# A 31-tap causal convolution with 16 taps on TensorE over stacked, shifted copies

## The chip, the cores and the metric

The kernel runs on one core of one Trainium2 chip. The metric is the device time in microseconds (us) of one execution. A core has TensorE (PE; its weight loads are shown apart as PEld), VectorE (DVE), ScalarE (ACT), GpSimd (POOL) and SyncE (SP). SP and ACT issue DMAs here. Engines wait for each other through semaphores only: `wait_ge(s, n)` holds an engine until semaphore `s` has reached `n`; a landed DMA adds 16, a finished instruction adds 1.

## The reference

Two decoder layers over 256 tokens of 1024 channels, all in float32. Layer 0 mixes tokens with a convolution module, layer 1 with sparse attention; each is followed by a mixture of 32 experts (two per token) and a gated embedding. The part that the change touches is the convolution module:

```python
def conv_module(xn, w_pw1, b_pw1, w_dw, b_dw, ln_g, ln_b, w_pw2, b_pw2):
    u = xn @ w_pw1 + b_pw1                     # 1024 -> 2048
    a, g = jnp.split(u, 2, axis=-1)
    u = a * jax.nn.sigmoid(g)                  # gated product
    u = lax.conv_general_dilated(              # 31 taps, each channel by itself
        u, w_dw[:, None, :].astype(u.dtype), window_strides=(1,),
        padding=[(CONV_WIDTH - 1, 0)], dimension_numbers=("NWC", "WIO", "NWC"),
        feature_group_count=u.shape[-1]) + b_dw
    u = jax.nn.silu(layer_norm(u, ln_g, ln_b))
    return u @ w_pw2 + b_pw2
```

## The kernel before

**Stages.** Norm of the input, conv module, mixture 0 with 32 experts of 6.3 MB each, embedding, attention, mixture 1, embedding. SP issues nearly all loads, in one order written out by hand; where a load goes over a buffer still in use, SP waits for its last reader. Each expert is three loads of 2 MB (gate, up, down) into one of two ring halves; inside the loop the gate and up loads wait for the gate and up products (`gu_mm`) of the expert before in that half, the down load for its down product (`y_mm`).

**Conv module.** Channels lie on partitions, in eight blocks of 128; tokens lie along the free axis. For each block c:
- PE computes pw1, 16 matmuls of 128x128 by 128x256 (L498). A float32 matmul shows as two records in the trace. After it, PE does the taps of block c-1 (`taps`, L477), and from block 3 on the channel sum of block c-3 (L483).
- ACT takes the sigmoid of the gate half (L1086) and builds six diagonal matrices, the identity times a tap weight (L1092).
- DVE forms the gated product into `cv0` (`glu`, L1324), a buffer with 30 columns of zeros in front, so that tap w of a block is a shifted view `cv0[:, c, w:w+256]`.
- The 31 taps are split. DVE does 20, each a multiply-add over a view, in two alternating accumulators (L1339, L1341, L1343). GpSimd does 5 (L990, L993, L994). PE does 6 (`PE_TAPS`), as matmuls with the diagonal matrices. DVE then adds the parts (L1353 to L1355).
- DVE's order is: taps of c, gated product of c+1, the adds of c (after PE's and GpSimd's parts), taps of c+1.

After block 7 PE puts the bias of pw2 into PSUM (L508, issued behind the last taps), finishes the channel sums and, with squares from ACT, the sums of squares (L513). DVE takes the mean at L1358. Then come square root, silu and pw2 (L522), 32 matmuls of 512 columns, and the router of mixture 0.

**The first loads.** SP: x; the vectors (biases, gains, the tap table `wdw_rows`, `bpw2`), which PE waits for before its first transposes (L461); pw1 in four parts (8 MB); pw2 (4 MB, L356); expert 0 (6 MB); after block 3 of pw1 two ple weights, after block 7 one attention weight and the gate weights of expert 1; after the last taps the embeddings; after pw2's products the up and down weights of expert 1. ACT first issues 14 small loads (router weights and biases, positions; L1066), then does its half of the norm (token tile 1; L1045, L1047, L1052).

## Time and profile before

| | us |
|---|---|
| median of 3 runs | 1414.63 (1410.31 to 1415.55) |
| the profiled execution | 1413.13 |
| its span | 1411.4 |
| PE busy | 1081.1 |
| DVE busy | 332.7 |
| ACT busy | 257.3 |
| POOL busy | 478.3 |

Mean DMA rate over the span: 318 GB/s, 447 MB read. The span is the time from the first to the last instruction of the profiled execution. In the rows below a timeline row gives start, duration, engine, line, operation, tiles and shapes and, in brackets, how long the engine stood idle before it and what ended that. "x32" means 32 instructions run together; their duration is that of the whole run. L numbers are lines of the kernel before.

### The profile page before, as it was taken

Reading aid. Unit: us, or ns where it says so; the run is one execution under the profiler, and the core shown is the slowest. Engines: PE = TensorE matmul, PEld = TensorE weight load, DVE = VectorE, ACT = ScalarE, POOL = GpSimd, SP = SyncE. Lnnn points to the kernel's source line nnn. Section 1 sums busy time; section 2 is a strip of 40 time slices with the busy share of each in tenths; the row PEclk is TensorE's granted clock in tenths of the full one; section 3 lists DMA queues with packets and bytes.
Section 4 is the critical chain, followed back from the end, with each engine's and each line's share of the span. In section 5 each row is a group of like instructions: output and inputs, shape, how many; then the busy total and the mean of one; then the engine's idle time right before and its main releaser. Section 6 shows DMA issues by size and latency. Waiting matters only on the chain.

```text
span 1411.4 us, 27617 instructions
## 1 busy us (share of the span) xinstructions
PE 1081.1 (77%) x10280; PEld 617.1 (44%) x10281; DVE 332.7 (24%) x917; ACT 257.3 (18%) x608; POOL 478.3 (34%) x793
## 2 busy tenths in 40 slices
PE   5985977776767777677999799877767677676768
PEld 4863454433433433343454554544334343333433
DVE  3997230000000000001407691300000000000011
ACT  2211131111111111111202481311111111111111
POOL 3663035334343343432000040363343333452520
PEclk9996989888888988888999899998988888888979
DMA  8922049999999999998303801799999999998940
GB/s 250 403 91 111 26 193 408 428 430 427 429 430 428 428 430 428 429 430 316 125 2 118 358 1 44 319 415 428 428 430 429 427 430 429 427 429 335 430 172 30
DMA packets 62731, 448.75 MB, mean 318 GB/s; under 512 B 10826, under 2 KB 21698, under 8 KB 38114
## 3 DMA queue, kind: packets, MB, share of 16 engines
q1 hardware_dynamic: 58114, 447.91, 76.5%
q10 hardware_dynamic: 4576, 0.30, 0.3%
q8 instruction: 26, 0.43, 0.1%
q14 instruction: 15, 0.12, 0.0%
HBM read 447.14 MB, written 1.05 MB: 318 GB/s over the span
## 4 chain that ended last, share of the span: by engine, by line
DMA 44%; PE 36%; DVE 6%; issue 3%; ACT 1%; SPq 1%; POOL 0%; DVEq 0%
DMA ring<-in_moe_w_up 42%; PE PS L547 14%; PE PS L437 9%; PE PS L522 2%; DMA ring<-in_moe_w_down 2%; PE PS L562 2%; PE PS L534 1%; PE PS L752 1%; PE PS L725 1%; PE PS L569 1%; SPq L310 1%; DVE ppw L1654 1%; PE PS L425 1%; PE PS L586 1%; DVE ppw L1679 1%
## 5 line engine op out<-in xcount | busy, mean ns | idle before, releaser
L547 PE MATMUL PS<-ring,arena 128*32 128x256 f32 x4128 | 347.4, 500 | 203.9 <-DMA ring<-in_moe_w_up 183.0
L547 PEld LDWEIGHTS PS<-ring,arena 128*32 128x32 f32 x4128 | 164.0, 138 | 376.4 <-issue 225.4
L1389 DVE TENSOR_TENSOR arena<-PS,arena 64x256 f32<-64x256 f32 x65 | 27.8, 428 | 634.7 <-ACT arena L1147 629.0
L562 PE MATMUL PS<-ring,arena 128*32 128x256 f32 x2080 | 125.7, 381 | 30.8 <-DVE arena L1392 30.8
L964 POOL TENSOR_SCALAR arena<-arena 128x32 f32<-128x32 f32 x64 | 18.8, 294 | 334.3 <-PE PS L534 330.8
L1147 ACT ACTIVATE arena<-PS 64x256 f32<-64x256 f32 x64 | 24.2, 378 | 546.6 <-PE PS L547 546.6
L923 POOL TENSOR_SCALAR arena<-arena 128x512 f32<-128x512 f32 x67 | 105.9, 1580 | 23.5 <-POOL arena L970 12.9
L562 PEld LDWEIGHTS PS<-ring,arena 128*32 128x32 f32 x2080 | 73.0, 109 | 61.2 <-issue 37.4
L917 POOL TENSOR_SCALAR arena<-arena 128x32 f32<-128x32 f32 x260 | 88.6, 364 | 13.1 <-POOL arena L964 12.9
L925 POOL TENSOR_TENSOR arena<-arena 128x512 f32<-128x512 f32 x67 | 85.3, 1273 | 5.6
L534 PE MATMUL PS<-hn,arena 128*32 128x256 f32 x1072 | 76.8, 399 | 8.4 <-DMA ring<-in_moe_w_down 7.8
L569 PE MATMUL PS<-arena 32*128 32x256 f32 x1040 | 74.5, 397 | 6.6 <-ACT arena L1145 0.6
L437 PE MATMUL PS<-wb,xnT 128*128 128x512 f32 x160 | 74.1, 621 | 0.0
L1384 DVE TENSOR_TENSOR arena<-PS,g 128x256 f32<-128x256 f32 x67 | 28.5, 425 | 177.9 <-PE PS L540 177.9
L912 POOL TENSOR_TENSOR rstd<-rstd,nhalf 128x1 f32<-128x1 f32 x12 | 8.2, 696 | 163.1 <-DVE rstd L1289 163.1
L970 POOL TENSOR_SCALAR arena<-arena 128x1 f32<-128x1 f32 x64 | 14.6, 228 | 138.3 <-PE PS L569 138.3
L569 PEld LDWEIGHTS PS<-arena 32*128 32x128 f32 x1040 | 50.3, 183 | 17.4 <-issue 17.4
L1151 ACT COPY arena<-PS 128x256 f32<-128x256 f32 x64 | 23.9, 374 | 162.9 <-PE PS L562 162.9
L534 PEld LDWEIGHTS PS<-hn,arena 128*32 128x32 f32 x1072 | 36.3, 110 | 35.2 <-issue 9.2
L927 POOL TENSOR_TENSOR arena<-arena 128x256 f32<-128x256 f32 x67 | 49.0, 731 | 5.2
L1147 ACT ACT_TABLE_LOAD x32 | 41.1, 1283 | 45.7 <-issue 45.7
L437 PEld LDWEIGHTS PS<-wb,xnT 128*128 128x128 f32 x160 | 31.6, 200 | 39.2 <-issue 39.2
(303 smaller groups left out, 1275.4 us busy)
## 6 DMA issues: line engine op xcount, KB each, us to landing
ring<-in_moe_w_up SPq DMA_DIRECT2D x64, 2048.0 KB, 23.1
ring<-in_moe_w_down SPq DMA_DIRECT2D x64, 2048.0 KB, 24.8
ring<-in_moe_w_gate SPq DMA_DIRECT2D x63, 2048.0 KB, 18.7
wb<-in_ple_w_gate SPq DMA_DIRECT2D x4, 2048.0 KB, 20.4
ring<-in_conv_w_pw SPq DMA_DIRECT2D x3, 2048.0 KB, 19.4
ring<-in_nsa_w_in SPq DMA_DIRECT2D x3, 2048.0 KB, 20.5
wb<-in_nsa_w_in SPq DMA_DIRECT2D x2, 2048.0 KB, 9.0
wb<-in_nsa_cmp_w SPq DMA_DIRECT2D x2, 2048.0 KB, 8.3
```

What stands on the lines that cost most here:

```text
L437: i = pe.matmul(PS[:, bank, :], lhs[:, k, t * P:(t + 1) * P], w[:, k, :], start=start and k == 0, stop=(k == KD - 1))
L522: i = pe.matmul(PS[:, 2 * n + t, :], cT[:, k, t * P:(t + 1) * P], dense(PW2[n])[:, k, :], start=False, stop=(k == KD - 1))
L534: i = pe.matmul(PS[32 * j:32 * j + 32, BGX, 0:Q4].rearrange("q (p c) -> q p c", c=2), lhs[:, t, :], rows[:, j], start=(t == 0), stop=(t == ...
L547: i = pe.matmul(PS[32 * j:32 * j + 32, BGU, 0:256].rearrange("q (p c) -> q p c", c=2), xT[:, k, :], w[:, k, :].rearrange("q (p h c) -> q h ...
L562: i = pe.matmul(PS[32 * j:32 * j + 32, BY, 0:Q4], hT[:, c, 32 * f:32 * f + 32], w_dn(s)[:, f, c, Q4 * j:Q4 * (j + 1)], start=(q == 0), sto ...
L569: i = pe.matmul(PS[:, ACC + j, 256 * t:256 * (t + 1)], w[32 * j:32 * j + 32, t * P:(t + 1) * P], ysb[32 * j:32 * j + 32, :], start=False, ...
L917: i = g.tensor_scalar(eq4[:, t, k, :], c32, S4[:, t, k:k + 1], None, ALU.is_equal)
L923: g.tensor_scalar(eqr, srow, cc, None, ALU.is_equal).then_inc(count, 1)
L925: g.tensor_tensor(eqr, eqr, wrow, ALU.mult).then_inc(count, 1)
L927: g.tensor_tensor(to, eqr[:, 0, :], eqr[:, 1, :], ALU.add).then_inc(ok, 1)
L1147: nc.scalar.activation(gs[64:128, :], PS[0:64, BGU, 0:256], ACT.Silu).then_inc(sil_ok, 1)
L1384: return v.tensor_tensor(dst.rearrange("p (j c) s -> p j c s", c=2), PS[:, BGX, Q4:Q4 + 256].rearrange("p (c j s) -> p j c s", c=2, j=4), ...
```

## The change

- `PE_TAPS` goes from 6 to 16, in stacks of 4 (`STACK`). GpSimd does no taps any more, and DVE does 15.
- For the taps on PE the gated product of a block is written by ACT to a DRAM tensor (`xdram`), ACT waits for that, and reads it back four times, each shifted by one token, so that 32 channels x 4 shifts fill the 128 partitions (`xst`, for four groups q of 32 channels). A matmul then has a 128x32 stationary matrix holding 4 taps of 32 channels, and writes 32 partitions; 4 groups x 4 runs make 16 matmuls for 16 taps of all 128 channels.
- The stationary matrices come from one GpSimd product per block (`stk` times `wst`), in place of ACT's six operations. Their tap weights are brought into stacked order once, through a second DRAM tensor (`wdram`).
- DVE adds two parts in place of three: first its two accumulators, then PSUM.
- In front, SP loads x, the vectors without `bpw2`, and pw1. pw2 goes out in four 1 MB pieces, each after the copies of one of the blocks 0 to 3 have landed; `bpw2` behind them. Expert 0 goes out after the copies of blocks 6 and 7 have landed, then the embeddings, the gate weights of expert 1, the two ple weights and the attention weight.
- ACT's small loads are issued behind the copies of blocks 2 to 5.
- PE waits for pw2 and `bpw2` before the bias matmuls, and for the embeddings with one semaphore.

```diff
-PE_TAPS, POOL_TAPS = 6, 5
+PE_TAPS, STACK = 16, 4
+RUNS = PE_TAPS // STACK
+DVE_TAPS = TAPS - PE_TAPS
+XW = T + STACK * (RUNS - 1)
...
+        xdram = nc.dram_tensor("glu_rows", (KD, P, T + STACK * RUNS - 1), F32, kind="Internal").ap()
+        wdram = nc.dram_tensor("tap_rows", (P, STACK * 8 * RUNS), F32, kind="Internal").ap()
...
             sp.dma_start(wdw_rows, conv_w_dw[0]).then_inc(vec_in, 16)
-            sp.dma_start(bpw2, conv_b_pw2).then_inc(vec_in, 16)
...
-            for n in range(2):
-                sp.dma_start(dense(PW2[n]), cols(conv_w_pw2[0], n)).then_inc(w2_in[n], 16)
+            for c in range(4):
+                sp.wait_ge(xst_in[c % 2], 16 * STACK * (c // 2 + 1))
+                n, hk = c // 2, slice(4 * (c % 2), 4 * (c % 2) + 4)
+                sp.dma_start(dense(PW2[n])[:, hk, :], cols(conv_w_pw2[0], n)[:, hk, :]).then_inc(w2_in[n], 16)
+            sp.dma_start(bpw2, conv_b_pw2).then_inc(w2_in[0], 16)
+            for c in range(6, KD):
+                sp.wait_ge(xst_in[c % 2], 16 * STACK * (c // 2 + 1))
             expert(0, 0, 0)
-
-            sp.wait_ge(pw1_mm, 4)
+            sp.wait_ge(conv_ok, KD)
+            embeddings(0)
+            sp.wait_ge(pw1_mm, 8)
+            gate_up_load(0, 1, R1[0], 0, gu_in[1])
             for n in range(2):
                 sp.dma_start(dense(WB[n]), cols(ple_w_gate[0], n)).then_inc(ple_in[n], 16)
-            sp.wait_ge(pw1_mm, 8)
             sp.dma_start(dense(WB[2]), cols(nsa_w_in[0], 2)).then_inc(in_in[2], 16)
-            gate_up_load(0, 1, R1[0], 0, gu_in[1])
-            sp.wait_ge(conv_ok, KD)
-            embeddings(0)
             sp.wait_ge(out_mm, 4)
...
             def taps(c):
-                pe.wait_ge(glu_ok, c + 1)
                 pe.wait_ge(dg_ok, c + 1)
                 if c >= 2:
                     pe.wait_ge(conv_ok, c - 1)
-                for i_ in range(PE_TAPS):
-                    w = TAPS - PE_TAPS + i_
-                    i = pe.matmul(PS[:, 4 + c % 2, 0:T], dgb[:, c % 2, i_, :], cv0[:, c, w:w + T],
-                                  start=(i_ == 0), stop=(i_ == PE_TAPS - 1))
+                pe.wait_ge(xst_in[c % 2], 16 * STACK * (c // 2 + 1))
+                for m in range(RUNS):
+                    for q in range(4):
+                        i = pe.matmul(PS[32 * q:32 * q + 32, 4 + c % 2, 0:T], dgb[c % 2][:, q, m, :],
+                                      xst[c % 2][:, q, STACK * m:STACK * m + T], start=(m == 0), stop=(m == RUNS - 1))
                 i.then_inc(tap_mm, 1)
...
             for n in range(2):
+                pe.wait_ge(w2_in[n], 48 - 16 * n)
                 for t in range(NT):
                     pe.matmul(PS[:, 2 * n + t, :], ones[0:1, :], bpw2[:, 512 * n:512 * (n + 1)], start=True, stop=False)
...
+            link(g.tensor_scalar(stk[:, :], iot[:, :], colp[:, 0:1], None, ALU.is_equal))
+            pool.wait_ge(wst_in, 16 * (1 + STACK))
             for c in range(KD):
-                pool.wait_ge(glu_ok, c + 1)
                 if c >= 2:
-                    pool.wait_ge(conv_ok, c - 1)
...
+                    pool.wait_ge(tap_mm, c - 1)
+                shape = [P, 4, RUNS, 32]
+                g.tensor_tensor(dgb[c % 2], stk[:, :].unsqueeze(1).unsqueeze(1).broadcast_to(shape),
+                                wst[:, :, c, :].unsqueeze(3).broadcast_to(shape), ALU.mult).then_inc(dg_ok, 1)
...
             norm(0, ROW_MIX)
+            act.wait_ge(vec_ok, 3)
+            act.dma_start(wdram, wch.rearrange("p j c m -> p (j c m)")).then_inc(wst_in, 16)
+            act.wait_ge(wst_in, 16)
+            for j in range(STACK):
+                act.dma_start(wst[32 * j:32 * j + 32, :, :, :].rearrange("p q c m -> p q (c m)"),
+                              wdram.rearrange("(q p) (j n) -> j p q n", q=4, j=STACK)[j]).then_inc(wst_in, 16)
             for c in range(KD):
                 act.wait_ge(pw1_mm, c + 1)
...
                 if c >= 2:
                     act.wait_ge(tap_mm, c - 1)
-                for i_ in range(PE_TAPS):
-                    w = TAPS - PE_TAPS + i_
-                    i = nc.scalar.activation(dgb[:, c % 2, i_, :], ident[:, :], ACT.Copy, scale=wdw[:, c, w:w + 1])
-                i.then_inc(dg_ok, 1)
+                act.wait_ge(glu_ok, c + 1)
+                act.dma_start(xdram[c], cv0[:, c, DVE_TAPS:]).then_inc(xst_out, 16)
+                act.wait_ge(xst_out, 16 * (c + 1))
+                for j in range(STACK):
+                    act.dma_start(xst[c % 2][32 * j:32 * j + 32, :, :],
+                                  xdram[c].rearrange("(q c) u -> c q u", q=4)[:, :, j:j + XW]).then_inc(xst_in[c % 2], 16)
+                small_loads(c)
...
                 dve.wait_ge(c_dve, own[0])
+                link(v.tensor_tensor(cT[:, c, :], cT[:, c, :], accb, ALU.add))
                 dve.wait_ge(tap_mm, c + 1)
-                dve.wait_ge(ptap_ok, c + 1)
-                link(v.tensor_tensor(accb[1], PS[:, 4 + c % 2, 0:T], pac[c % 2], ALU.add))
-                link(v.tensor_tensor(cT[:, c, :], cT[:, c, :], accb[0], ALU.add))
-                v.tensor_tensor(cT[:, c, :], cT[:, c, :], accb[1], ALU.add).then_inc(conv_ok, 1)
+                v.tensor_tensor(cT[:, c, :], PS[:, 4 + c % 2, 0:T], cT[:, c, :], ALU.add).then_inc(conv_ok, 1)
```

## Rows read from the trace of the kernel before

**Rows 1.** The page's chain that ended last, shares of the span by line

```profile
DMA ring<-in_moe_w_up 42%; PE PS L547 14%; PE PS L437 9%; PE PS L522 2%; DMA ring<-in_moe_w_down 2%; PE PS L562 2%; PE PS L534 1%; PE PS L752 1%; PE PS L725 1%; PE PS L569 1%; SPq L310 1%; DVE ppw L1654 1%; PE PS L425 1%; PE PS L586 1%; DVE
```

**Rows 2.** Timeline of SP's issues around the start of mixture 0

```profile
172.80 0.34 SPq L310 DMA_DIRECT2D ring<-in_moe_w_up  x1
...
202.03 0.35 SPq L310 DMA_DIRECT2D ring<-in_moe_w_gate  x1
```

**Rows 3.** Timeline of the conv module, blocks 2 and 5 to 6

```profile
46.78 7.07 PE L498 MATMUL PS<-xnT,wb 128*128 128x256 f32 x32
...
89.42 0.47 DVE L1324 SCALAR_TENSOR_TENSOR ppw<-PS,vecT,arena 128x256 f32<-128x256 f32 x1
...
89.94 2.86 PE L477 MATMUL PS<-ppw,arena 128*128 128x256 f32 x12 [2.27 <-DVE ppw L1324]
...
92.64 0.59 PE L483 MATMUL PS<-hn,ones 128*128 128x256 f32 x2
...
99.91 0.47 DVE L1343 SCALAR_TENSOR_TENSOR arena<-ppw,arena 128x256 f32<-128x256 f32 x1
...
100.30 0.47 DVE L1343 SCALAR_TENSOR_TENSOR hn<-ppw,arena,hn 128x256 f32<-128x256 f32 x1
...
101.88 0.47 DVE L1324 SCALAR_TENSOR_TENSOR ppw<-PS,vecT,arena 128x256 f32<-128x256 f32 x1
```

**Rows 4.** Groups by line and shape: total busy us, mean ns, idle time before

```profile
L1343 DVE SCALAR_TENSOR_TENSOR arena<-ppw,arena 128x256 f32<-128x256 f32 x72 | 45.1, 626 | 0.0
...
L925 POOL TENSOR_TENSOR arena<-arena 128x512 f32<-128x512 f32 x67 | 85.3, 1273 | 5.6
```

**Rows 5.** Timeline of the first expert of mixture 0, on PE

```profile
197.96 3.86 PE L547 MATMUL PS<-ring,arena 128*32 128x256 f32 x64 [1.85 <-issue]
...
203.72 1.94 PE L562 MATMUL PS<-ring,arena 128*32 128x256 f32 x32 [0.48 <-DVE arena L1392]
...
205.58 0.51 PE L540 MATMUL PS<-ident,arena 128*128 128x128 f32 x2
```

**Rows 6.** The chain in order of time, a later expert: start us, us, what

```profile
261.67 6.35 PE PS L547 x64
```

**Rows 7.** DMA issues of the last 20 us: count, KB each, us to landing

```profile
out_h<-h SPq DMA_DIRECT2D x2, 512.0 KB, 2.6
```

**Rows 8.** Timeline of the front

```profile
2.00 2.14 ACTq L1066 DMA_DIRECT2D rowb<-in_moe_b_rg  x1
...
6.47 1.23 DVE L1285 CUSTOM_DVE_ANT_0 hn<-h 128x1024 f32<-128x1024 f32 x1 [6.32 <-DMA h<-in_x]
...
6.99 5.72 ACTq L1066 DMA_DIRECT2D posi<-in_positions  x6
...
12.74 1.28 ACT L1045 ACT_TABLE_LOAD   x1 [12.59 <-issue]
...
15.40 0.38 PE L461 MATMUL PS<-ident,arena 88*128 88x88 f32 x1 [15.40 <-DMA arena<-in_conv_b_pw]
...
20.39 14.46 PE L498 MATMUL PS<-xnT,wb 128*128 128x256 f32 x64
```

**Rows 9.** Windows: length, busy per engine, PE clock, DMA share, GB/s

```profile
10.00:12.00 2.00, 0.00 (x0) 0.00 (x0) 0.00 (x0) 0.00 (x0) 0.00 (x0) 1.00 0.26 57
...
110.00:112.00 2.00, 0.00 (x0) 0.00 (x0) 2.00 (x5) 0.00 (x0) 0.88 (x2) 0.50 0.94 401
```

**Rows 10.** DMA queues over 0 to 30 us; issues of 6.4 to 7 us

```profile
q10 hardware_dynamic: 4576, 0.30, 13.4%
...
wb<-in_conv_w_pw SPq DMA_DIRECT2D x2, 512.0 KB, 10.4
```

**Rows 11.** Timeline of the end of the convolution

```profile
120.28 3.91 PE L508 MATMUL PS<-arena,ones 1*128 1x512 f32 x8
...
129.67 0.42 DVE L1358 TENSOR_SCALAR arena<-PS 128x256 f32<-128x256 f32 x1 [1.38 <-PE PS L483]
...
131.06 6.78 PE L513 MATMUL PS<-xnT,ones 128*128 128x256 f32 x16 [1.50 <-ACT xnT L1096]
```

More of the change, by code:

```diff
@@ L103, in build @@
         colp = sb("colp", [P, 1])
+        stk = sb("stk", [P, 32])
         xtot = sb("xtot", [P, 1])
         tab = sb("tab", [P, 2, NE], I32)
-        A = sb("arena", [P, 4424])
+        A = sb("arena", [P, 4400])
         off = [0]
@@ L112, in carve @@
             off[0] += n
-            assert off[0] <= 4424, off[0]
+            assert off[0] <= 4400, off[0]
             return A[:, a:a + n]
@@ L196, in build @@
         wdw = carve(8 * TAPS).rearrange("p (c w) -> p c w", c=8)
-        accb = [carve(256) for _ in range(2)]
-        dgb = carve(2 * PE_TAPS * P).rearrange("p (b i q) -> p b i q", b=2, i=PE_TAPS)
-        pac = [ppw[:, 2304:2560], ppw[:, 2560:2816]]
-        ptm = ppw[:, 2816:3072]
+        accb = carve(256)
+        wch = carve(STACK * 8 * RUNS).rearrange("p (j c m) -> p j c m", j=STACK, c=8)
+        wst = carve(8 * 4 * RUNS).rearrange("p (q c m) -> p q c m", q=4, c=8)
+        xst = [x_.rearrange("p (q u) -> p q u", q=4) for x_ in (ppw[:, 2304:2304 + 4 * XW], carve(4 * XW))]
+        dgb = [x_.rearrange("p (q m s) -> p q m s", q=4, m=RUNS) for x_ in (ppw[:, 3392:3392 + 512], carve(512))]
         bpw2 = carve(1024)[0:1, :]
@@ L252, in build @@
         ple_in = [sem(f"ple_in{i}") for i in range(2)]
-        proj_in = sem("proj_in")
-        att_in, gate_in, mask_ok = sem("att_in"), sem("gate_in"), sem("mask_ok")
-        tap_mm, dg_ok, ptap_ok, root_in, root_ok = sem("tap_mm"), sem("dg_ok"), sem("ptap_ok"), sem("root_in"), sem("root_ok")
+        att_in, gate_in = sem("att_in"), sem("gate_in")
+        tap_mm, dg_ok, wst_in, root_in, root_ok = sem("tap_mm"), sem("dg_ok"), sem("wst_in"), sem("root_in"), sem("root_ok")
+        xst_in, xst_out = [sem(f"xst_in{i}") for i in range(2)], sem("xst_out")
         x_bld = sem("x_bld")
@@ L980, in _ @@
             g.tensor_scalar(thr[:, :], iot[:, 1:8], float(SLOTS), None, ALU.mult).then_inc(const_ok, 1)
+            link(g.tensor_scalar(stk[:, :], iot[:, :], colp[:, 0:1], None, ALU.is_equal))
+            pool.wait_ge(wst_in, 16 * (1 + STACK))
             for c in range(KD):
-                pool.wait_ge(glu_ok, c + 1)
                 if c >= 2:
-                    pool.wait_ge(conv_ok, c - 1)
-                for i_ in range(POOL_TAPS):
-                    w = TAPS - PE_TAPS - POOL_TAPS + i_
-                    u = cv0[:, c, w:w + T]
-                    if i_ == 0:
-                        g.tensor_scalar(pac[c % 2], u, wdw[:, c, w:w + 1], None, ALU.mult).then_inc(c_pool, 1)
-                        own[0] += 1
-                    else:
-                        link(g.tensor_scalar(ptm, u, wdw[:, c, w:w + 1], None, ALU.mult))
-                        i = g.tensor_tensor(pac[c % 2], pac[c % 2], ptm, ALU.add)
-                        if i_ < POOL_TAPS - 1:
-                            link(i)
-                i.then_inc(ptap_ok, 1)
-                pool.wait_ge(ptap_ok, c + 1)
+                    pool.wait_ge(tap_mm, c - 1)
+                shape = [P, 4, RUNS, 32]
+                g.tensor_tensor(dgb[c % 2], stk[:, :].unsqueeze(1).unsqueeze(1).broadcast_to(shape),
+                                wst[:, :, c, :].unsqueeze(3).broadcast_to(shape), ALU.mult).then_inc(dg_ok, 1)
             rsqrt(3, rstd[:, 1, 0:1])
@@ L1332, in _ @@
                     dve.wait_ge(tr_ok, 4)
-                nv = TAPS - PE_TAPS - POOL_TAPS
-                for w in range(nv):
-                    o = cT[:, c, :] if w % 2 == 0 else accb[0]
+                for w in range(DVE_TAPS):
+                    o = cT[:, c, :] if w % 2 == 0 else accb
                     u = cv0[:, c, w:w + T]
```

51 lines of the change are left out of this document (28 added, 23 removed).

## Prediction

> **What bounds the kernel now.** I read the page's chain first. Its largest item is DMA for the experts' up weights, 42% of the span [rows 1]: both mixture stages are paced by weight loads. The change touches none of them, so a gain has to come from starting that stage sooner. SP issues the last up load of the first two experts at 172.80 us, when the conv module's last product ends, and the next gate load only at 202.03 us, when the first expert's gate and up products (L547) are done [rows 2]. Both are released by compute, and the 4.2 MB issued at 172.8 need 11 us at the 401 GB/s of [rows 9], not the 29 between, so whatever the conv module saves passes one for one into the end of the span.
>
> Inside the conv module I read one channel block (there are eight) in the timeline. The gated product of one block (L1324) starts at 89.42 us, the next at 101.88 us: a period of 12.46 us [rows 3]. VectorE has no gap in it. PE has: the taps (L477) start after 2.27 us of waiting for VectorE. PE's own work in a period is 7.07 us for pw1, 2.86 for the taps and 0.59 for the channel sum, 10.5 us. VectorE is the bound: 24 instructions, 18 of them L1343. That group's mean is 626 ns, while two neighbours late in a block, after GpSimd has finished, start 0.39 us apart [rows 3, 4]. The page names no cause; both engines read SBUF in the slow part.
>
> **Part 1, taps.** VectorE goes from 20 taps to 15 and from three combining adds to two; GpSimd's nine operations per block give way to one product. Per block: 15 x 0.39 = 5.9, the gated product 0.4, two dependent adds 0.9 (each a little over the 0.39, as it waits for the one before), so 7.2 us. GpSimd's new operation is a 128x512 tensor_tensor, 1.27 us [rows 4]; while it runs VectorE's slower rate costs at most 0.6 us. VectorE: 7.8 us.
>
> PE: 6 taps as full matmuls (12 records, 2.86 us) become 16 matmuls with a 128x32 stationary tile, 32 records in four column groups. The same form is L547: 64 records in 3.86 us, and 6.35 us for an expert that follows a long wait for DMA [rows 5, 6]. So 32 records cost 1.93 us, or 3.2 us after a long idle time. Per block 7.07 + 1.93 + 0.59 = 9.6 us. **PE takes over as the bound at 9.6 us**, if the copies keep up.
>
> A rule speaks against it: the Trainium skill (TensorEngine Tiling, "Key Properties") says that changing the tiling mode drains the TensorE, and the change makes two such switches per block. The trace shows no price: L562, in 32-wide tiles, ends at 205.66 us and the full transpose L540 starts at 205.58 [rows 5]. It is put at nothing.
>
> **Part 2, the copies.** Each block's gated product is written to DRAM by ACT, waited for, and read back four times, shifted. Call L the time from the gated product to the last read landed. No row shows such a round trip. Nearest rows: the output's 512 KB write lands 2.6 us after issue [rows 7]; ACT's position loads took 5.72 / 6 = 0.95 us each to issue in the crowded front [rows 8]. Low: 0.4 + 2.2 + 4 x 0.35 + 2.2 = 6.2 us. High: 1 + 3.5 + 3.8 + 4 = 12.3 us. I take 0.5 + 2.6 + 4 x 0.45 + 2.6 = 7.5 us, since DMA is all but idle there after the change (the pw2 pieces go out one at a time, after a block's copies have landed).
>
> Is it covered? PE runs pw1 of block c+1 (ending at E), then the taps of c. Sigmoid and gated product follow 1 us after E, and the taps of block c+1 are due at E + 9.6. So L is hidden up to 8.6 us. ACT is in order: waiting for its write and issuing reads, it stands about L - 2.5 = 5 us behind each product; queued behind is the next sigmoid, due 8.6 us after. That also fits. Blocks 2 and 3 add ACT's router loads, four each, of which one took 2.14 us to issue in the front [rows 8], blocks 4 and 5 the positions; of this most fits in the 3 us that ACT has left per block, and I put 1 us for all, bounds 0 and 6.
>
> **Part 3, the front.** Now ACT issues small loads until 12.7 us, and only then starts its half of the norm (table load 12.74 us); PE's first transposes wait for the vectors until 15.40 us and pw1 starts at 20.39 us [rows 8]. The small loads are 4576 packets and take 13.4% of 30 us of all engines, 4.0 us each [rows 10]. Without them ACT's norm can start at 6.3 us (x has landed) and be done by about 12. The vectors then set the start: 15.4 - 4.0 = 11.4; I take 12.0, since between 10 and 12 us the engines are only 26% busy [rows 9], so not all of the delay is queueing. Bounds: 15.4 (no gain) and 8. pw1 starts 5 us after the vectors: **17.0 us instead of 20.4**. Its first weights landed at 6.5 + 10.4 = 16.9 us [rows 10], minus the same 4.0 is 12.9: in time.
>
> Why not 8: by the Trainium skill (DMA: Bandwidth & Descriptors, "Why a DMA increments its semaphore by 16 and not by 1") a load of 31 partitions runs on one engine, and the tap table is such a load; at that page's 27 GiB/s its 124 KB would take, as an estimate, 4.4 us, landing near 12. The trace's low rate at 10 to 12 us, 57 GB/s [rows 9], agrees.
>
> **Part 4, the start of the loop.** pw1(0) and pw1(1) run from 17.0 to 31.2. The gated product of block 0 is out at 25.2 (sigmoid right after pw1(0), ACT having issued the tap-weight reads by then). Its copies meet the pw1 stream, which runs to about 36: L = 9 there, landing 34.2, so PE stands 3 us (bounds 0 and 6). GpSimd's tap matrices need the tap weights through DRAM too, issued at about 18.5: 2.6 + 1.8 + 2.6 later, plus 1.3, is 26.8, in time. Then pw1 ends: 34.2 + 1.9 + 7.1 = 43.2 for block 2, 52.2, and four blocks at 9.6: 90.6 for block 7; with the 1 us for small loads 91.6.
>
> **Part 5, the tail, now exposed.** The last copies have no cover: 91.6 + 1 + 7.5 = 100.1. PE has idled about 6 us, and the clock of such stretches falls to 0.50 (110 to 112 us) [rows 9]. taps(7) 1.9 to 3.2, I take 2.6: 102.7. Behind them in PE's order stand the eight bias records, 3.91 us [rows 11], hidden before under VectorE's last block, and three channel sums at 0.6: 106.6, 108.4. The mean (L1358) starts at 108.5; before 129.67 [rows 11]: **21.2 us sooner**. The 16 squares ran at half clock, 6.78 us [rows 11]; at pw1's full-clock rate (32 records in 7.07 us) they need 3.5. PE has now been busy for 8 us just before, so I take back 1.8 (bounds 0 and 3.3).
>
> **Part 6, the loads moved back.** The first expert's three loads, the embeddings, the gate of expert 1, two ple weights and one attention weight (16.0 MB) now start at about 100 us: at 401 GB/s 40 us [rows 9], all down by 143. The embeddings, behind 6.3 MB, land near 121; PE wants them at about 143. The first expert is wanted at 175. The next issue, at 172.8 - 23 = 150, finds an empty queue. Nothing binds, with 7 us at the tightest place; the cost is zero. pw2's last piece goes out after block 3's copies, near 62 us, 45 us ahead of use; the wait on it, moved ahead of the bias products, costs nothing.
>
> **Sum.** -21.2 - 1.8 = -23 us. The profiled run took 1413.13 us (span 1411.4), 1.5 us under the median of 1414.63: 1413.1 - 23 = **1390 us**.
>
> **Rivals.**
> The round trip paces the loop (L from 9 to 13). For L over 8.6 blocks come every (10.6 + L) / 2, because PE holds the next pw1 back behind the taps. At L = 11: 10.8 us, 1.2 x 6 = 7, the tail 3.5 and the start 2 more: 1403; at 12.3, 1408. For it: nothing shows such a chain yet, and ACT's slow issues. Against: the issues were slow in a crowd that is gone.
> The other side, slower: ACT's own order decides. It holds sigmoid(c+1) back until its reads are out, so blocks come every L - 1.5 once L passes 11. Block 7's copies then land at 25.2 + 7(L - 1.5) + L; with L = 13.5 that is 122.7 and the mean starts at 131, level with before; from there each us of L costs 8. At L = 15 the time is about 1424. It needs each of five transfers to take twice what [rows 7] shows.
> The four column groups do not overlap here: then 32 records take 7.1 us, blocks 14.8, and the time is near 1450. L547, the same form, speaks against.
> A larger gain: the vectors land at 8, the first copies in time, the clock holds in the tail: 3.4 + 3 + 1.5, and L = 6 another 1.5: about 1380.
>
> **How the numbers follow.** Forecast (1383 to 1399) 0.62; larger gain 0.12; round trip paces 0.16; slower by ACT's order 0.08; no overlap 0.02. The range reaches from the full gain to the round trip at its high bound: 1379 to 1407. About 0.5%, 7 us, is what a measurement of this kernel can tell from no change. The upper third of the pacing rival and the near end of the slower one fall within it, 0.07; slower keeps 0.08; faster 0.85.
>
> **What the new profile would show.** L498's first start at 17 (front). Its x32 groups 9.6 us apart with no gap before L477's successor (PE bound); gaps there mean the round trip. The time from a gated product to the taps that need it, for block 7, is L plus 0. The new tap group at 60 ns a record. The mean's start at 108, the first expert's L547 at 175, and SP's next gate load at 179 against 202.03: the last must equal the whole gain. If the last start moves by 23 and the time does not, the claim that compute releases the expert loads is wrong.

## The result, and the profile after

The changed kernel ran at 0.9948 of the time of the one before, with a 95% interval of 0.9931 to 0.9965: 1405.5 us against 1414.6 us by the medians, some 7.4 us by the ratio. Run again as it is, beside other runs, it gave 0.9963 (0.9945 to 0.9981), some 5.2 us. Forecast were 23 us. The direction was right, and a quarter to a third of the size came. One of the twelve executions of the kernel before took 4554 us and is not counted in the ratio. The profiled execution of the changed kernel, 1412.1 us, was the slowest of its twelve; the repeat was profiled at 1406.7, near its median.

First the route of the gain through the span. Each column is a start time in us, read from a timeline; "forecast" is worked out from the prediction's own steps.

| what starts | before | forecast | after | after, again |
|---|---|---|---|---|
| pw1 (L507) | 20.39 | 17.0 | 18.09 | 18.38 |
| taps of block 0 | | 34.2 | 41.75 | 40.99 |
| taps of block 7 (its copies have landed) | | 100.1 | 110.24 | 110.43 |
| mean (L1370) | 129.67 | 108.5 | 123.97 | 120.88 |
| SP's up load at the end of the conv module | 172.80 | 149.8 | 164.47 | 162.89 |
| SP's next gate load, in mixture 0 | 202.03 | 179.0 | 193.49 | 191.89 |
| first gate load released in mixture 1 | 880.1 | 857.1 | 871.5 | 870.0 |
| last gate load | 1320.4 | 1297.4 | 1318.4 | 1313.7 |

At the mean's start 21.2 us were forecast and 5.7 came, so 15.5 us are missing there, inside the convolution (12.4 in the repeat). What is left at SP's loads, about 8.5 us (10 in the repeat), is carried unchanged through mixture 0 and the whole attention layer. After that, in mixture 1, 6.6 us of it are lost in the first execution and 3.3 in the repeat.

The timeline of the changed kernel at its start (start, duration, engine, line, operation, tiles; in brackets the idle time before, and what ended it; a group that runs on past the end of a view is shown with the part that the view holds, as the x6 here):

```profile
13.10 0.38 PE L470 MATMUL PS<-ident,arena 88*128 88x88 f32 x1 [13.10 <-DMA ppw<-in_conv_w_dw]
...
18.09 2.23 PE L507 MATMUL PS<-xnT,wb 128*128 128x256 f32 x6
...
27.69 0.48 DVE L1339 SCALAR_TENSOR_TENSOR ppw<-PS,vecT,arena 128x256 f32<-128x256 f32 x1 [9.74 <-ACT arena L1096]
...
28.21 0.34 ACTq L1101 DMA_DIRECT2D glu_rows<-ppw  x1
...
33.86 1.77 ACTq L1104 DMA_DIRECT2D ppw<-glu_rows  x4
...
41.75 3.64 PE L486 MATMUL PS<-ppw 128*32 128x256 f32 x32 [8.91 <-DMA ppw<-glu_rows]
```

The gated product of block 0 starts at 27.69. ACT issues the write at 28.21 and may issue the reads only at 33.86, when the write has landed: 5.7 us for 139 KB (128 rows of 271 numbers). The reads take until 41.75. The whole way, L in the prediction, is 14.0 us, and PE stands 8.91 us before the taps (line L486). The gated product itself was held up by ACT: after the reads of the tap weights (issued until 25.9) it still had to load its table for the sigmoid, 1.28 us. In the kernel before that load lay in ACT's idle time, at 21.57.

The middle of the loop, blocks 2 to 4:

```profile
62.11 1.93 PE L486 MATMUL PS<-ppw 128*32 128x256 f32 x32
62.80 0.48 DVE L1339 SCALAR_TENSOR_TENSOR ppw<-PS,vecT,arena 128x256 f32<-128x256 f32 x1 [1.00 <-ACT arena L1096]
...
63.98 0.70 PE L492 MATMUL PS<-hn,ones 128*128 128x256 f32 x2
...
72.72 0.48 DVE L1339 SCALAR_TENSOR_TENSOR ppw<-PS,vecT,arena 128x256 f32<-128x256 f32 x1 [1.96 <-ACT arena L1096]
...
72.92 1.93 PE L486 MATMUL PS<-arena 128*32 128x256 f32 x32 [1.33 <-DMA arena<-glu_rows]
...
74.95 1.05 POOL L998 TENSOR_TENSOR arena<-stk,arena 128x512 f32<-128x512 f32 x1 [9.75 <-PE PS L486]
```

16 taps take 1.93 us on PE, DVE now has gaps, and GpSimd's product takes 1.05 us. Where the copies are in time no wait stands before the taps. Before those of block 3 there are 1.33 us and before those of block 4 1.10: L was 10.1 and 10.8 us there (62.80 to 72.92 and 72.72 to 83.49), with the router's small loads and the positions on ACT's queue and a piece of pw2 on SP's beside the copies.

The tail, where [rows 11] showed the bias matmuls at 3.91 us under the last taps of DVE:

```profile
102.97 0.48 DVE L1339 SCALAR_TENSOR_TENSOR ppw<-PS,vecT,arena 128x256 f32<-128x256 f32 x1 [1.43 <-ACT arena L1096]
...
110.24 3.64 PE L486 MATMUL PS<-arena 128*32 128x256 f32 x32 [5.39 <-DMA arena<-glu_rows]
...
113.81 7.19 PE L518 MATMUL PS<-arena,ones 1*128 1x512 f32 x8
...
120.93 2.93 PE L492 MATMUL PS<-hn,ones 128*128 128x256 f32 x6
...
123.97 0.42 DVE L1370 TENSOR_SCALAR arena<-PS 128x256 f32<-128x256 f32 x1 [9.54 <-PE PS L492]
```

And the same kernel by windows of 5 us (length, then busy time of PE, PEld, DVE, ACT, POOL, the granted clock of PE, DMA share, GB/s):

```profile
105.00:110.00 5.00, 0.00 (x0) 0.00 (x0) 5.00 (x14) 0.00 (x0) 0.00 (x0) 0.83 0.46 110
110.00:115.00 5.00, 4.76 (x34) 2.25 (x35) 1.49 (x4) 0.00 (x0) 0.00 (x0) 0.50 0.79 282
115.00:120.00 5.00, 5.00 (x8) 1.82 (x6) 0.00 (x0) 0.00 (x0) 0.00 (x0) 0.50 1.00 419
120.00:125.00 5.00, 3.86 (x8) 1.85 (x6) 0.99 (x3) 0.11 (x1) 0.00 (x0) 0.50 1.00 429
```

PE stands for five microseconds while it waits for the last copies. Then taps, bias and sums run one after another with the clock granted at 0.50, that is 1.2 GHz, and DVE does nothing but wait for them. From landing to mean: 13.7 us.

### The profile page after: what moved, and what is told of

It is laid out like the page before. It is cut to its first block, busy times and chain, and to the rows that moved or that the text cites. A ratio compares the mean times of both kernels' runs of the same rounds, so it can differ in the third digit from the quotient of the medians.

```text
span 1409.9 us, 27825 instructions
## 1 busy us (share of the span) xinstructions
PE 1073.7 (76%) x10440; PEld 605.7 (43%) x10441; DVE 292.5 (21%) x870; ACT 243.3 (17%) x560; POOL 426.0 (30%) x731
## 4 chain that ended last, share of the span: by engine, by line
DMA 47%; PE 40%; DVE 6%; issue 4%; SPq 1%; ACT 1%; ACTq 1%; POOL 0%; DVEq 0%
DMA ring<-in_moe_w_up 42%; PE PS L556 14%; PE PS L447 9%; PE PS L531 2%; PE PS L507 2%; DMA ring<-in_moe_w_down 2%; PE PS L571 2%; DMA glu_rows<-ppw 1%; PE PS L543 1%; PE PS L761 1%; PE PS L734 1%; PE PS L435 1%; PE PS L486 1%; PE PS L578 1%; SPq L318 1%
```

## Experiments: where the conv module's gain went

**The kernel unchanged, again.**

> The changed kernel, unedited, as the base of the next three and for a second profile. The first profile shows the first expert's products of mixture 0 8.5 us sooner than before, the start of mixture 1 8.6 us sooner, but the end only 1.5 us sooner. Theory A (the stands of PE inside the first two experts of a mixture differ from run to run): the front repeats to 0.5 us, the end moves by several us against the first profile, and the ratio to before is 0.994 to 0.996. Theory B (the change itself costs 6 us in mixture 1): the start of mixture 1 is again 8.6 us sooner and the end again 1.5 us.

0.9963 (0.9945 to 0.9981). The tail came out shorter in this execution: bias 4.19 us in place of 7.19, mean at 120.88. So single profiled executions of this program differ by some 3 us there, and what follows is compared with both. Neither theory came out whole: the front did not repeat to 0.5 us (SP's gate load 1.6 us sooner), and the last gate load was 6.7 us sooner than in the kernel before in place of 2.0.

**The copies of block 0 against the stream of pw1.** The last four megabytes of pw1 go out only after block 0's copies have landed.

```diff
             for i, (c0, c1) in enumerate(PW1_PARTS):
+                if i == 3:
+                    sp.wait_ge(xst_in[0], 16 * STACK)
```

> The last part of pw1 (4 MB) is issued only after the copies of block 0 have landed. Theory (the first copies are slow because they share the DMA engines with SP's stream of pw1): block 0's way from gated product to landed copies falls from 14.0 us to 7 to 8, PE's stand before the first taps from 8.9 to about 2.5, and these taps run at full clock (1.9 instead of 3.6 us); block 1's copies now meet the stream and cost back up to 4 us; net 3 to 8 us sooner than the changed kernel. Rival (the first copies are slow for another reason, such as first use of the DRAM tensor or ACT's order): 14 us again, and no gain; pw1's block 4 may even wait for its weights, up to 5 us later.

Measured: 0.9944 (0.9925 to 0.9963), no different from the changed kernel, where 3 to 8 us were expected. The timeline of this kernel says why:

```profile
29.27 0.34 ACTq L1103 DMA_DIRECT2D glu_rows<-ppw  x1
31.12 1.76 ACTq L1106 DMA_DIRECT2D ppw<-glu_rows  x4
35.48 1.93 PE L488 MATMUL PS<-ppw 128*32 128x256 f32 x32 [1.98 <-DMA ppw<-glu_rows]
36.39 0.39 ACTq L1103 DMA_DIRECT2D glu_rows<-ppw  x1
...
53.76 3.64 PE L488 MATMUL PS<-arena 128*32 128x256 f32 x32 [9.25 <-DMA arena<-glu_rows]
```

Without the stream beside it the write takes 1.9 us in place of 5.7 and L is 6.7 us (28.76 to 35.48) in place of 14.0; PE stands 1.98 us. The four megabytes then go out together, and block 1's copies meet them: 17.9 us (product at 35.89, landed at 53.76), a stand of 9.25 us, where up to 4 us more had been expected. That the stream is what makes the copies slow is shown; the remedy only moves the collision by one block.

**The other direction: more stream beside the copies.** SP's waits ahead of pw2 and of expert 0 are taken out, so that these loads follow pw1 at once, as in the kernel before.

```diff
             for c in range(4):
-                sp.wait_ge(xst_in[c % 2], 16 * STACK * (c // 2 + 1))
                 n, hk = c // 2, slice(4 * (c % 2), 4 * (c % 2) + 4)
...
-            for c in range(6, KD):
-                sp.wait_ge(xst_in[c % 2], 16 * STACK * (c // 2 + 1))
             expert(0, 0, 0)
```

> The changed kernel with one part undone: pw2 and the first expert go out behind pw1 without waiting for any copies, as before the change. Theory (the copies share the DMA engines with SP's stream): each copy that meets the stream, until about 55 us, takes 14 to 18 us, so blocks 0 to 3 come every 13 us or more and pw1 ends 10 to 20 us later than in the changed kernel, near 115 us; the time is 1413 to 1425. Rival (only the first copies are slow, whatever SP does): pw1 ends within 3 us of the changed kernel's 110 us.

1.0066 (1.0043 to 1.0089): slower than the kernel before, 17 us behind the change. Its PE rows (the last group, of 32, goes on past the view's end):

```profile
43.63 3.64 PE L483 MATMUL PS<-ppw 128*32 128x256 f32 x32 [10.29 <-DMA ppw<-glu_rows]
...
47.20 7.34 PE L504 MATMUL PS<-xnT,wb 128*128 128x256 f32 x32
...
68.44 1.94 PE L483 MATMUL PS<-arena 128*32 128x256 f32 x16 [13.90 <-DMA arena<-glu_rows]
```

L is 16.3 us for block 0 (27.36 to 43.63) and 32.5 for block 1 (35.96 to 68.44), twice what was expected; blocks 2 to 6 come without a stand. The moved loads, then, are no side matter of the change. They carry it: with 16 taps on PE and these two loads in front the kernel loses.

**The order of the tail.** Bias matmuls and the sums of blocks 5 and 6 are put ahead of the taps of block 7, into PE's wait for the last copies.

```diff
-            taps(KD - 1)
+            pe.wait_ge(glu_ok, KD)
             for n in range(2):
                 pe.wait_ge(w2_in[n], 48 - 16 * n)
                 ...
-            for c in range(KD - 3, KD):
+            for c in range(KD - 3, KD - 1):
                 channel_sum(c)
+            taps(KD - 1)
+            channel_sum(KD - 1)
```

> PE's order at the end of the convolution: the bias matmuls and the channel sums of blocks 5 and 6 go ahead of the taps of block 7, into the 5.4 us in which PE waits for the last copies. Theory (the tail is exposed and at half clock): 7.2 us of bias and 2 of the 2.9 us of sums leave the path, the taps of block 7 run near full clock; the mean comes 8 to 10 us after the copies' landing less, so 8 to 10 us sooner. Rival (the tail is bound by the copies and DVE, not PE): the mean moves by less than 3 us.

0.9872 (0.9845 to 0.9899), 1393.9 us: 18 us under the kernel before, 11 to 13 under the change by the two ratios. PE in this kernel:

```profile
105.13 3.70 PE L518 MATMUL PS<-arena,ones 1*128 1x512 f32 x8
108.75 1.95 PE L492 MATMUL PS<-hn,ones 128*128 128x256 f32 x4
110.63 2.75 PE L486 MATMUL PS<-arena 128*32 128x256 f32 x32
114.01 0.70 PE L492 MATMUL PS<-hn,ones 128*128 128x256 f32 x2 [0.63 <-DVE hn L1369]
```

The copies have landed by 110.45, when SP sends out the load that waits for them too, and the mean starts at 114.82: 4.4 us from landing to mean in place of 13.7 or 10.4. SP's gate load goes out at 183.8, which is 9.7 or 8.1 us sooner than in the change.

**The clock by itself.** Same order as in the change, but 11 matmuls that nobody reads fill PE's wait before the last taps.

```diff
+            for _ in range(11):
+                pe.matmul(PS[:, 7, 0:T], ones[:, :], xnT[:, 0, :], start=True, stop=True)
             taps(KD - 1)
```

> The order stays; eleven matmuls whose result nobody uses (4.9 us at full clock) fill PE's wait for the last copies. It tells the clock from the order. Clock theory: taps of block 7 take 1.9 instead of 3.6 us, the bias 3.9 instead of 7.2, the sums 1.8 instead of 2.9, the mean comes 5 to 6 us sooner. Rival (bias matmuls with one row are slow by themselves): no change, or 0.5 us later.

0.9933 (0.9911 to 0.9955). Its rows, and its windows from 110 us on:

```profile
109.14 1.93 PE L486 MATMUL PS<-arena 128*32 128x256 f32 x32 [0.62 <-DMA arena<-glu_rows]
111.01 3.70 PE L520 MATMUL PS<-arena,ones 1*128 1x512 f32 x8
114.63 1.56 PE L492 MATMUL PS<-hn,ones 128*128 128x256 f32 x6
...
117.69 3.72 PE L525 MATMUL PS<-xnT,ones 128*128 128x256 f32 x16 [1.50 <-ACT xnT L1111]
```

```profile
110.00:115.00 5.00, 5.00 (x30) 2.22 (x23) 0.51 (x2) 0.00 (x0) 0.00 (x0) 1.00 0.98 357
115.00:120.00 5.00, 3.50 (x17) 2.76 (x16) 3.19 (x9) 2.76 (x8) 0.00 (x0) 1.00 1.02 436
```

The clock stays at 1.00 (2.4 GHz), and landing to mean takes 7.2 us: the clock is worth 3.2 to 6.5 us there (10.4 and 13.7 less 7.2), the order of the work the other 3 (7.2 less 4.4; its windows from 105 to 115 us show 0.89 and 0.77, so it had not the full clock). The sums of squares fall from 5.4 to 6.1 us to 3.72 as well. From landing to SP's up load at the end of the module the change takes 54.2 and 52.5 us, this kernel 46.0 and the new order 44.3: measured to there, the clock gives most of what the order gives.

In the timed runs much less is left of it. The median, 1402.9, is 4 us under the repeat of the change, which ran beside it, and the ratio 2 us under that of the first measurement (0.9948); the intervals overlap with both. The profiled execution, 1396.5, was the fastest of the six. One difference to the new order shows in the profile: this program has eleven matmuls more, and stands of PE in the mixtures, of which the next section tells, sum to 18.2 us in place of 12.0. So the effect of the clock on the tail is shown, its worth in the timed median is not.

**ACT's small loads in front, as before.**

```diff
+            for c in range(2, 6):
+                small_loads(c)
             norm(0, ROW_MIX)
...
-                small_loads(c)
```

> The changed kernel with the other part of the load order undone: ACT issues its 14 small loads first, as before the change. Theory: the vectors land at about 15.4 instead of 13.1 us and pw1 starts at 20.4 instead of 18.1; blocks 2 to 5 no longer carry these loads, so PE's stands of 1.3 and 1.1 us before the taps of blocks 3 and 4 go away; the net is within 1 us. Rival: the start does not move, because the tap table on few engines sets it.

A single execution took 1405.7 us. The tap table lands at 14.52 in place of 13.10 and pw1 starts at 19.51 in place of 18.09; block 0's taps stand 11.23 us in place of 8.91, while those of blocks 3 and 4 wait 0.29 and 0.62 in place of 1.33 and 1.10. SP issues its gate load at 193.4, as in the change (193.5). But the tail ran at the clock of the repeat here (bias 4.15 us, there 4.19), and against the repeat pw1, the mean and the gate load are all late by 1.1 to 1.5 us (19.51, 122.30 and 193.4 against 18.38, 120.88 and 191.9). So the move of the small loads is worth about 1.4 us, and that lasts. It is one execution: in the ten profiled ones whose front is that of the change the table landed anywhere from 13.10 to 14.15, so the effect may be as small as 0.4 us.

**pw1 in pieces.** With the order of the tail kept, pw1's blocks 4 to 7 and then pw2 go out in one-megabyte pieces, one after each block's copies; a second kernel also puts ACT's small loads behind the last SiLU.

```diff
+            for i, (c0, c1) in enumerate(PW1_PARTS[:3]):
+                pw1_part(i, c0, c1)
+            for c in range(KD):
+                sp.wait_ge(xst_in[c % 2], 16 * STACK * (c // 2 + 1))
+                if c < 4:
+                    pw1_part(c, 4 + c, 5 + c)
+                else:
+                    n, hk = (c - 4) // 2, slice(4 * (c % 2), 4 * (c % 2) + 4)
+                    sp.dma_start(dense(PW2[n])[:, hk, :], ...).then_inc(w2_in[n], 16)
```

> The tail in the new order, and in front only the first half of pw1 goes out as a stream; the blocks 4 to 7 of pw1 and then pw2 go out in 1 MB pieces, one behind each block's copies. Theory (a stream of more than 1 MB costs one block's copies 7 to 10 us each, a single piece 1 to 2): block 0's copies take 6.7 us, block 1's 8 to 9, PE stands 2 us and at most 2 us before the first two taps, and the end of pw1 comes 7 to 9 us sooner than in the changed kernel; with the tail's 8 to 10 us the time is about 1385. Rival (any load beside a copy costs it the same): block 1's copies take 14 us or more and the gain over the tail order alone is under 2 us.

> The order of the tail and the pw1 pieces as in the run with both, and ACT's fourteen small loads not between the copies of blocks 2 to 5 but after the last SiLU of the conv module, where ACT has nothing to do. Theory A (copies share their queue with whatever ACT issues, and the engines with SP's stream): blocks 2 to 5 lose their stands of about 2 us each, the conv module ends 4 to 6 us earlier than with the small loads among the copies, time 1388 to 1391. Rival: each block is bound by PE by then, and the stands only move: 1393 to 1395.

0.9869 (0.9842 to 0.9895) and 0.9896 (0.9867 to 0.9924): neither beats the order of the tail alone, 0.9872, where about 1385 and 1388 to 1391 us were expected. In the first, block 0's taps stand 1.46 us at 34.82 in place of 8.91 at 41.75, but those of blocks 1 to 3 stand 1.73, 1.87 and 2.02, each beside a piece of pw1 and two of them beside the router's small loads, and of the 7 us won 3 are left at SP's gate load (180.7 against 183.8). Those 3 us include 0.9 by which pw1 itself began sooner (18.25 against 19.15). With the small loads moved as well the mean starts at 112.40, no sooner than with the pieces alone (111.66; 114.82 with the order of the tail alone), and the gate load goes out at 183.0. The collision can be spread; less than half of it is got back, and none of that is seen in the timed median.

## Experiments: what is lost again in mixture 1

In mixture 1 of the changed kernel PE stands in the gate and up products of the first experts, and the view names no releaser ("issue"). First the changed kernel:

```profile
899.77 4.72 PE L556 MATMUL PS<-ring,arena 128*32 128x256 f32 x49 [2.24 <-issue]
916.49 5.75 PE L556 MATMUL PS<-ring,arena 128*32 128x256 f32 x64 [6.47 <-issue]
```

Then the kernel before in the same stretch:

```profile
915.08 1.97 PE L547 MATMUL PS<-ring,arena 128*32 128x256 f32 x26 [0.98 <-issue]
920.89 2.24 PE L547 MATMUL PS<-ring,arena 128*32 128x256 f32 x35 [3.85 <-issue]
```

From the first released gate load of mixture 1 to the fourth into the ring, 54.3 us pass in the kernel before, 61.7 in the one after and 58.9 in its repeat. Nothing that the change touches runs there. What does differ is the number of instructions ahead of the loop in PE's program: the change adds ten matmuls per block, 80 in all. So I added 80 small ones to the kernel before, which do no work:

```diff
                 i.then_inc(tap_mm, 1)
+                for _ in range(10):
+                    pe.matmul(PS[0:32, 7, 0:1], ones[:, 0:32], ones[:, 0:1], start=True, stop=True)
```

> The kernel before, with 80 small matmuls more on PE (ten behind each block's taps, a 128x32 stationary tile and one column, result unused), about as many PE instructions as the change adds; they fall into PE's 2 us of waiting per block. Theory (PE's stands in the first experts of mixture 1 come from loading its instructions and depend on where the loop lies in the program): the front stays (SP's gate load at 202 us), the stands of mixture 1's first three experts grow from 6.8 us in total to about 11, with one of 6 to 7 us before the second expert, and the end comes 4 to 5 us later than before. Rival (the stands are the change's doing in some other way, its DMAs or its earlier timing): the stands stay at 6.8 us and the time within 1 us of before.

```profile
923.69 5.76 PE L549 MATMUL PS<-ring,arena 128*32 128x256 f32 x64 [6.96 <-issue]
```

The stand of 6 to 7 us is there, and the stretch takes 61.6 us, as in the changed kernel. The 4 to 5 us expected at the end did not come in the timed runs: 1.0013 (0.9991 to 1.0034); the profiled execution, 1418.9, was the slowest of its twelve. With 5 and with 20 per block, then the first of these once more, then 40 such matmuls in PE's wait for the first SiLU, in the changed kernel and in the one with the new tail:

> The kernel before with 40 small matmuls on PE in the conv module (five per block, nobody reads them), half as many as in the run with 80. There the stands of PE in the expert products of the first experts of mixture 1, for which the trace names no releaser, grew from 3.8 to 7.0 us for the largest, and the stretch from the first issue of that mixture's expert loads to the fourth grew from 54.3 us (879.0 to 934) to 61.6 us. Theory P: what counts is how many instructions lie ahead of the loop in PE's program, so the number changes the stands: the largest of mixture 1 is neither 3.8 nor 7.0 us but another value, and the stretch lies somewhere from 50 to 62 us by the place. Rival D: the stands came from the draw of the run (where the transfers happen to stand when PE enters the loop) and have no tie to the count: then 54.3 or 61.6 us, either, and nothing that follows the count. Time within 0.5% of the kernel before by both.

> The kernel before with 160 small matmuls on PE in the conv module, twenty per block. Theory P (place in PE's program): the stands of the first experts of both mixtures move again, to other values than with none (5.8 us the largest in mixture 0, 3.8 in mixture 1) and with 80 (3.2 and 7.0). Rival D: no pattern with the count. The 160 matmuls themselves cost about 160 x 0.06 = 10 us of PE over eight blocks; PE waits 2.3 us and more per block for the gated product before, so at most some 3 us of that reach the end. Time 1413 to 1420.

> The kernel before with 40 small matmuls in the conv module once more. The first time it was timed at 0.9959 [0.9941, 0.9977] of the kernel before, with no work taken away. By theory P this repeats, 0.994 to 0.998, and the sum of its stands over 2 us stays near 9.5 us against 13.6 in the kernel before; by rival D it comes back to 0.998 to 1.002.

> The changed kernel with 40 small matmuls that nobody reads, put on PE behind the sums of squares, where PE waits some 4 us for ACT's first SiLU, so that they cost nothing by themselves (40 x 0.06 = 2.4 us). Theory P (what lies ahead of the expert loop in PE's program moves PE's stands without releaser in it): the sum of the stands over 2 us from the first expert on, 17.9 and 15.1 us in two profiled executions of the changed kernel and 13.6 in the kernel before, is another, and the time is another than 1405 to 1407 by up to 6 us either way. Rival D (draw of the run): sum 15 to 18 us and time 1404 to 1408.

> The tail order (bias matmuls and sums of blocks 5 and 6 ahead of the taps of block 7) with the same 40 small matmuls behind the sums of squares. By theory P the stands over 2 us (3.0, 6.8 and 2.1, together 12.0 without them) change, and the time lies within 6 us of 1393.9; by rival D nothing changes: 1392 to 1396. By both it stays well ahead of the changed kernel, 1388 to 1400.

Measured; "stands" are PE's idle times of 2 us and more without a named releaser from 130 us on, from one profiled execution each, in the order mixture 0 | first experts of mixture 1 | its end:

| kernel | small matmuls | ratio to before (95%) | stands, us | sum |
|---|---|---|---|---|
| before | 0 | 1 | 5.8 \| 3.9 \| 3.9 | 13.6 |
| before | 40 | 0.9959 (0.9941 to 0.9977) | 4.8 \| 4.7 \| none | 9.5 |
| before | 40, again | 0.9974 (0.9962 to 0.9987) | 5.0 \| 5.6 \| 2.1 | 12.7 |
| before | 80 | 1.0013 (0.9991 to 1.0034) | 3.2 \| 2.2, 7.0 \| 3.7 | 16.2 |
| before | 160 | 0.9982 (0.9963 to 1.0002) | 4.4 \| 3.0, 6.4 \| none | 13.8 |
| after | 0 | 0.9948 (0.9931 to 0.9965) | 5.6 \| 2.2, 6.5 \| 3.5 | 17.9 |
| after | 0, again | 0.9963 (0.9945 to 0.9981) | 5.3 \| 7.0 \| 2.7 | 15.1 |
| after | 40 | 0.9959 (0.9944 to 0.9974) | 5.1, 6.3 \| 2.7 \| 2.6 | 16.7 |
| tail order | 0 | 0.9872 (0.9845 to 0.9899) | 3.0 \| 6.8 \| 2.1 | 12.0 |
| tail order | 40 | 0.9909 (0.9887 to 0.9932) | 4.7, 4.8 \| 2.9 \| 2.8 | 15.2 |
| filled wait | 11 | 0.9933 (0.9911 to 0.9955) | 3.1, 3.6 \| 3.4, 5.2 \| 2.9 | 18.2 |

What follows. The stands go with the program: in the kernel before 40 matmuls give nearly the same stands in mixture 0 and 1 twice, 80 bring back in mixture 1 the pattern of the changed kernel, and in the changed kernel 40 more move the large one from mixture 1 to mixture 0. In all eight traces of the change and its variants without added matmuls the largest stand of mixture 1 is 6.4 to 7.0 us; with 11 added it is 5.2, with 40 it is 2.7 and 2.9. The time moves too, though not with the sum of the stands. The kernel before with 40 useless matmuls was measured faster twice, both intervals clear of 1. With 160 its median was 1408.8, where 1413 to 1420 were expected. The tail order with 40 was 5.6 us slower by the medians (1399.5 against 1393.9), with intervals that just overlap; in its profile SP's gate load of mixture 0 goes out 6.1 us later (189.9 against 183.8), behind a new stand of 4.7 in the first expert, while its up load before that is late by only 0.9. The size of the stands is not settled by the count alone: the same program differs by 3 us in the sum from one execution to the next, the expectation that the sum of the second run stays near 9.5 failed (12.7), and the 40 in the changed kernel moved nothing in the median where up to 6 us were allowed.

What PE waits for can be read in the DMA records. Every page lists a queue q8 of the kind "instruction"; here it is for the kernel before, then with 80 and with 160 added matmuls (packets, MB, share):

```profile
q8 instruction: 26, 0.43, 0.1%
```

```profile
q8 instruction: 28, 0.46, 0.1%
```

```profile
q8 instruction: 29, 0.48, 0.1%
```

The 40 matmuls give 27 both times; the changed kernel and all its variants, those with 11 and 40 added too, give 28. In the kernel before only PE's program grows with the added matmuls, while the other queue of this kind, q14, keeps its 15 packets. So q8 carries PE's instructions, in pieces of 16 KB. They come only in the first passes: in the changed kernel none starts between 240 and 650 us or between 960 and 1330, inside the loops. And in the sixteen traces each of the 53 stands of 2 us and more ends 1.2 to 1.7 us after such a piece has landed. In the stand from 910.02 to 916.49 of the changed kernel the piece is recorded from 913.96 to 914.91; in the one from 917.04 to 920.89 of the kernel before, from 918.54 to 919.45. Within those windows the engines are busy with expert weights (99% on SP's queue from 910 to 917). So PE stands there until its own next instructions have come. How long before its record a piece was asked for, and why it comes up to 4.5 us into a stand, no trace shows; that it waits behind the weights is likely and was not tested. No run moved a piece on purpose and left the program's length alone.

## Why the prediction was wrong

- **What bounds the kernel.** Held. The conv module was the place to gain, DVE its bound before and PE after. "One for one" held from SP's load at the end of the module (8.3 us sooner) through the first release in mixture 1 (8.6 us sooner), 700 us later. It failed in mixture 1, by 6.6 us in one profiled execution and 3.3 in the other (last gate load 2.0 and 6.7 us sooner). The prediction named no such term; the only wait of PE marked "issue" in its rows is one of 1.85 us [rows 5]. What the runs showed is that PE waits for pieces of its own program in the first experts, and that 80 more matmuls shift where.
- **Part 1, taps.** Held: 1.93 us for 32 records, the rate of L547 [rows 5]; no drain seen, as a full-tile channel sum starts at 63.98 before the 32-wide taps end at 64.04. Ends of matmuls are modelled, but the starts say the same: from the taps of block 5 to those of block 6 9.40 us pass (92.89 to 102.29), no more than the 9.6 of the three parts, with both switches in them. The drain between tiling modes of which the Trainium skill tells (TensorEngine Tiling, "Key Properties") costs nothing here that the rows show, as was put. Blocks 2 to 7 came every 9.8 us on average (53.83 to 102.97 in five steps) against 9.6.
- **Part 2, copies.** Held where they run alone: 7.3 us in the tail (102.97 to 110.24) and 6.7 in block 0 of the kernel with late pw1, against 7.5.
- **Part 3, front.** Tap table at 13.10 against 12.0 (the estimate from the Trainium skill, DMA: Bandwidth & Descriptors, also was near 12), pw1 at 18.09 against 17.0: 1.1 us short. With the small loads in front the table came 0.4 to 1.4 us later, not 4.0. The share of the engines that their packets took was read as a delay of the other loads, and most of it was none. What brought the rest (15.40 to 14.52) was not tried apart; the load of `bpw2`, which also left the front, is the other difference there.
- **Part 4, the start of the loop: the first step that failed.** L = 9 for copies beside the pw1 stream, with PE standing 0 to 6 us. It was 14.0, with a stand of 8.9. The product was ready 2.5 us late (27.69 against 25.2: 1.1 from the front, the rest ACT's table load for the sigmoid, 1.28 us, which had no term), GpSimd's first matrices came at 34.9 in place of 26.8 (their tap weights had landed only at 32.1), hidden behind the copies, the taps started 7.6 us late, and after the long wait these taps and the next pw1 ran slower (3.64 and 7.89 us for 1.93 and 7.17), another 2.4. By the last product the module is 10.4 us late. The terms of L came from a write at the quiet end of the program [rows 7] and from issue times; the expectation that the same transfers cost only 1.5 us more beside a full stream was the error, and even the high bound of 12.3 lay below. With the last 4 MB of the stream held back L was 6.7, with 10 MB more in front 16.3.
- **Part 5, the tail: the second.** From landing to mean 8.4 us were put (2.6 + 3.91 + 1.8), 13.7 and 10.4 were measured. The list of what lay there was right, its clock was not: bias and sums were priced from a row at the higher clock, though the same paragraph let PE stand for six microseconds before them. The runs showed the granted clock at 0.50 from 110 to 125 us, and 7.2 us from landing to mean once the wait was filled. That the bias matmuls could lie ahead of the wait was not seen either. The squares and the rest up to pw2's end gave 2.6 us against 1.8.
- **Part 6, loads moved back.** Held: SP's up load goes out at 164.47 and the last of the moved loads is issued by 138. What it missed is the other side: pw2 and expert 0 left in front cost 17 us.
- **The rivals.** The time lies where the pacing rival put it (1403 to 1408), for another reason, and that is luck: L passed 8.6 us by much only in the first blocks (14.0 in block 0; 10.1 and 10.8 in blocks 3 and 4, which cost 2.4 us), while that rival had six blocks paced by it, and 5.3 us of what is missing lie in the tail. ACT's order did not decide: in block 1 ACT waited from 36.77 to 41.95 for its write to land, and then again for PE.

The sum: of 23 us, 10.4 are lost in the first blocks less 0.2 for the shorter last copies, 5.3 in the tail, 0.8 come back in the squares. That leaves 8.3, which is what SP's loads show (10 in the repeat, whose tail was shorter). Of it mixture 1 takes 6.6 us in the first profile and 3.3 in the second. The first of these executions was the slowest of its twelve, and the timed ratios leave 5 to 7 us; so the loss there is more likely 1 to 5 us in most executions, which is an estimate from the difference and was not measured.

## What to carry to other kernels

A step that PE waits for moves the work behind it onto the end: first list what stands behind the wait in PE's order and needs nothing from it, put that ahead, and price the rest at the clock of an engine that has just stood still. Here that was worth 11 to 13 us, more than the change itself, and 7 us between the two programs with 40 added matmuls (0.9909 against 0.9959). A small copy that others wait for is priced beside the traffic that really runs then, and an edit of under 0.5% that alters the length of an engine's program is compared with one of equal length before its gain is believed.

## What the runs showed of the hardware that was not expected

- A write of 139 KB and four reads, in sequence on ACT's queue, took 6.7 to 7.3 us alone, 14.0 and 17.9 us while SP's queue streamed 4 MB, and 16.3 and 32.5 us with 10 MB more in front. One megabyte beside each block's copies left stands of 1.7 to 2.0 us in blocks 1 to 3.
- After 5 us without work PE ran at a granted clock of 0.50 for the next 15 us (0.66, 0.68 and 0.50 in the second execution), although it was busy for 13.6 of them; after the same wait filled with useless matmuls it stayed at 1.00.
- Forty matmuls without work, added early in PE's program, shortened a 1414 us kernel by 0.26 to 0.41%. All 53 stands of 2 us and more without a named releaser ended 1.2 to 1.7 us after a 16 KB piece on the queue q8 "instruction" had landed, and its pieces grew from 26 to 29 with 160 matmuls more.
